# MLP up projection as seven half-size products a block, in blocks of 256 features, in a one-core trunk kernel

## What is computed

```python
z = rmsnorm(h, norm_mlp[l])                                     # 1024 x 1024
h = h + jnp.square(jax.nn.relu(z @ w_up[l])) @ w_down[l]        # w_up 1024 x 4096, w_down 4096 x 1024
...
return rmsnorm(h, norm_final)
```

## Time and profile before

| | |
|---|---|
| median of 3 runs | 1613.97 us |
| the profiled execution, its own time | 1612.35 us |
| its span in the profile | 1610.6 us |
| TensorE busy | 1550.3 us, 96% |
| VectorE, ScalarE, GpSimd busy | 756.5, 276.2, 408.2 us |
| the MLP's up and down matmuls | 3072, from about 896 to 1594 us |
| mean granted clock of TensorE | 0.989 of full speed |

### The profile page before, as it was taken

How to read it: one execution, slowest core, us unless ns; L and a number is a source line. 1 busy time by engine, 2 the same in 40 slices (tenths; PEclk the granted TensorE clock), 3 DMA queues, 4 the chain that set the end, 5 groups by cost and what they waited for, 6 DMA issues and landing times.

```text
span 1610.6 us, 20783 instructions
## 1 busy us (share of the span) xinstructions
PE 1550.3 (96%) x7608; PEld 1298.4 (81%) x7608; DVE 756.5 (47%) x1630; ACT 276.2 (17%) x575; POOL 408.2 (25%) x239
## 2 busy tenths in 40 slices
PE   5996999999999999999999999999999999999996
PEld 4785787878898988878888888888888888888884
DVE  6787665553564646476516622222232222222225
ACT  4120111220222222231102310101020101010013
POOL 1331132321010101104333306060513333240602
PEclk9997999999999999999999999999999999999998
DMA  5442344345211110103541103020211111020202
GB/s 167 117 120 72 93 117 119 105 158 164 72 41 39 34 44 26 53 27 125 170 170 53 53 1 105 0 92 13 65 39 52 52 47 58 26 78 0 91 0 104
DMA packets 93314, 119.16 MB, mean 74 GB/s; under 512 B 23504, under 2 KB 57424, under 8 KB 93264
## 3 DMA queue, kind: packets, MB, share of 16 engines
q1 hardware_dynamic: 62416, 78.49, 15.8%
q10 hardware_dynamic: 30848, 40.00, 7.8%
HBM read 96.57 MB, written 20.97 MB: 73 GB/s over the span
## 4 chain that ended last, share of the span: by engine, by line
PE 88%; DVE 7%; SPq 2%; issue 1%; ACT 1%; DMA 1%; ACTq 1%; POOL 0%; DVEq 0%
PE acc L497 27%; PE acc L499 27%; PE acc L498 27%; SPq L342 1%; PE aux L741 1%; DVE tb L1527 1%; PE aux L735 1%; PE aux L744 1%; DMA stage<-in_w_in 1%; PE aux L628 1%; ACTq L966 1%; PE aux L634 1%; DVE y_raw L1549 0%; SPq L339 0%; DVE tb L1574 0%
## 5 line engine op out<-in xcount | busy, mean ns | idle before, releaser
L421 POOL CAST w_hi<-stage 128x1024 fp32r<-128x1024 f32 x102 | 117.5, 1152 | 801.6 <-PE acc L499 674.3
L425 POOL TENSOR_TENSOR w_lo<-stage,w_hi 128x1024 fp32r<-128x1024 f32 x102 | 255.2, 2502 | 14.2 <-DVE x_in L1261 6.1
L497 PE MATMUL acc<-m_hi,w_hi 128*128 128x512 f32 x512 | 199.4, 390 | 0.0
L499 PE MATMUL acc<-m_hi,w_lo 128*128 128x512 f32 x512 | 199.2, 389 | 0.0
L498 PE MATMUL acc<-m_lo,w_hi 128*128 128x512 f32 x512 | 199.2, 389 | 0.0
L497 PE MATMUL acc<-w_hi,hid_hi 128*128 128x512 f32 x512 | 199.2, 389 | 0.0
L498 PE MATMUL acc<-w_lo,hid_hi 128*128 128x512 f32 x512 | 199.2, 389 | 0.0
L499 PE MATMUL acc<-w_hi,hid_lo 128*128 128x512 f32 x512 | 199.2, 389 | 0.0
L1797 DVE TENSOR_TENSOR h_res<-h_res,acc 128x512 f32<-128x512 f32 x128 | 87.9, 687 | 228.9 <-PE acc L499 228.9
L497 PE MATMUL acc<-w_hi,z_hi 128*128 128x256 f32 (+1 forms) x512 | 188.9, 369 | 0.0
L497 PE MATMUL acc<-z_hi,w_hi 128*128 128x512 f32 x448 | 179.8, 401 | 8.4 <-DVE z_lo L1221 5.0
(11 more groups left out here) (252 smaller groups left out, 2277.5 us busy)
## 6 DMA issues: line engine op xcount, KB each, us to landing
stage<-in_w_up SPq DMA_DIRECT2D x32, 512.0 KB, 3.7
stage<-in_w_down SPq DMA_DIRECT2D x32, 512.0 KB, 3.3
stage<-in_w_in SPq DMA_DIRECT2D x28, 512.0 KB, 3.8
gate_dram<-gate_t ACTq DMA_DIRECT2D x32, 256.0 KB, 2.0
x_in<-in_x SPq DMA_DIRECT2D x8, 512.0 KB, 8.1
stage<-in_w_in SPq DMA_DIRECT2D x32, 128.0 KB, 2.6
stage<-in_w_in SPq DMA_DIRECT2D x16, 256.0 KB, 3.1
gb_t<-gate_dram ACTq DMA_DIRECT2D x16, 256.0 KB, 3.1
```

The lines of the kernel that those rows point to most:

```text
L421: nc.gpsimd.tensor_copy(dst_hi, stage[:, s, :]).then_inc(hi_pool, 1)
L425: nc.gpsimd.tensor_tensor(dst_lo, stage[:, s, :], dst_hi.bitcast(F32), ALU.subtract)\
L497: nc.tensor.matmul(out, s_hi, m_hi_, start=first, stop=False)
L499: return nc.tensor.matmul(out, s_lo, m_hi_, start=False, stop=last)
```

## The change

Blocks are of 256 features, 16 in number. The first two are done in the plain way (4 up groups of 24 matmuls, 16 down groups of 6). The other 14 make the up projection by Strassen's seven products in Winograd's form: the z matrix is cut in four (feature half x position half), the weights of a block in four (feature half x 128 columns), and seven products of 512 x 128 x 512 (4 steps, 12 matmuls each) take the place of eight.

Sums of z quarters (S1 to S4) are made once: VectorE forms them during plain block 0 (`form_s1` to `form_s4`, each in two halves `u`), ScalarE casts and VectorE subtracts their parts during plain block 1. S1 takes the place of one quarter in `m_hi`, `m_lo`; the others lie where the weights of earlier stages were. Sums of weight quarters are made for each block by GpSimd, in `stage` and `t_sum`, and each of the seven weight operands (`piece`) is cast and subtracted into one of three slots of `t_hi`, `t_lo`. Product i goes to bank i % 4 of `aux`. ScalarE copies product 1 out; VectorE adds the others up in `tmp` and `c_tmp`, which gives four hidden quarters v, w, u, x in this order. The relu and the square become one VectorE operation. The down projection takes the positions' second half first (`DOWN_ORDER`).

The w_down part has buffers of its own (`dw_hi`, `dw_lo`); the same two slots of `stage` serve w_up and w_down. Waits: a piece waits for the product that used its slot; SyncE asks for w_down's halves after piece 4 and piece 7; the next block's w_up halves are asked for after w_down's halves are split.

The diff, cut to its core. The sizes and the order:

```diff
-FB = 512
+FB = 256
+N_PLAIN = 2
+DOWN_ORDER = (4, 5, 6, 7, 0, 1, 2, 3)
...
```

SyncE's loads of a seven-product block:

```diff
+            def load_block(g, first):
+                for i in range(2):
...
+                        sp.wait_ge(dn_ready, g * 2 + (i - 1))
+                    sp.dma_start(stage[:, i, :].rearrange("p (k c) -> p k c", k=KH),
+                                 w_up[:, KH * i:KH * i + KH, bass.ds(g * FB + N_PLAIN * FB, FB)]).then_inc(raw[i], 16)
+                for j in range(2):
+                    sp.wait_ge(t_ready, g * 7 + (4 if j == 0 else 7))
+                    sp.dma_start(stage[:, j, :].rearrange("p (k c) -> p k c", k=FT),
+                                 w_dn[:, bass.ds(g * FT + N_PLAIN * FT, FT), j * HALF:(j + 1) * HALF])\
+                      .then_inc(raw[j], 16)
...
```

GpSimd's part:

```diff
+                def piece(i, src):
+                    slot = i % 3
+                    pool.sem_inc(tick_pool, 1)
+                    pc.link(nc.gpsimd.tensor_copy(t_hi[:, slot, :, :], src))
+                    nc.gpsimd.tensor_tensor(t_lo[:, slot, :, :], src, t_hi[:, slot, :, :].bitcast(F32), ALU.subtract)\
+                      .then_inc(t_ready, 1)
+                pool.wait_ge(raw[0], g * 32 + 16 * (seen + 1))
+                pc.link(nc.gpsimd.tensor_tensor(b12, b12, b11, ALU.subtract))
...
+                piece(0, b11)
+                piece(1, t_sum[:])
...
+                piece(2, b11)
...
+                pool.wait_ge(prod, g * 7 + 1)
+                piece(3, b12)
+                pool.wait_ge(prod, g * 7 + 2)
+                piece(4, t_sum[:])
+                pool.wait_ge(prod, g * 7 + 3)
+                piece(5, b22)
+                pool.wait_ge(prod, g * 7 + 4)
+                piece(6, b21)
+                for j in range(2):
+                    pool.wait_ge(raw[j], g * 32 + 16 * (seen + 2))
...
+                    pc.link(nc.gpsimd.tensor_copy(hi, stage[:, j, :]))
+                    nc.gpsimd.tensor_tensor(lo, stage[:, j, :], hi.bitcast(F32), ALU.subtract).then_inc(dn_ready, 1)
...
```

TensorE's part:

```diff
+            def down(n0, h0, waits, order):
+                for j in range(2):
+                    for p, c in enumerate(order):
+                        n = n0 + 8 * j + p
+                        pe.wait_ge(out_free, n - 3)
+                        if j == 0 and p % 4 == 0:
+                            pe.wait_ge(lo_done, h0 + 2 + p // 2)
+                        if p == 0:
+                            pe.wait_ge(*waits[j])
...
+            def plain_block(f):
...
+                        if f == 0 and n in (OUT_MLP + 1, OUT_MLP + 2):
                             turn_z2(NCH - 3 + n - OUT_MLP)
-                        if half == 1 and q == 0:
+                        if f == 0 and half == 1 and q == 0:
                             pe.wait_ge(lo_done, SP_Z2 + 16)
...
+            def win_block(g, first):
...
+                for i, name in enumerate(("A11", "S2", "S3", "S1", "A22", "S4", "A12")):
+                    pe.wait_ge(t_ready, g * 7 + (i + 1))
+                    if i == 4:
+                        pe.wait_ge(p1_in, g + 1)
+                    if i > 4:
+                        pe.wait_ge(taken, g * 7 + (i - 4))
+                    for k in range(KH):
+                        mm = three(aux[:, i % 4, :], t_hi[:, i % 3, k, :], t_lo[:, i % 3, k, :],
+                                   a[name][0][:, k, :], a[name][1][:, k, :], k == 0, k == KH - 1)
+                    mm.then_inc(prod, 1)
...
```

VectorE's part (the sums of z, their place in plain block 0, and a block's adds, squares and low parts):

```diff
+            def form_s1(u):
+                link(V.tensor_tensor(raw_pair(s1_sum, u), z_pair(m_hi, 0, 1, u), z_pair(m_hi, 1, 1, u), ALU.add))
+                link(V.tensor_tensor(raw_pair(s_part, u), z_pair(m_lo, 0, 1, u), z_pair(m_lo, 1, 1, u), ALU.add))
+                V.tensor_tensor(raw_pair(s1_sum, u), raw_pair(s1_sum, u), raw_pair(s_part, u), ALU.add).then_inc(s_raw, 1)
...
+            def plain_block(f):
...
+                    if f == 0 and n < 2:
+                        form_s1(n)
+                    if f == 0 and n >= 2:
+                        form_s2(n - 2)
...
+                for j, p in down(n0 + 4, range(NCH)):
+                    if f == 0 and p % 4 == 3:
+                        (form_s3, form_s4)[j](p // 4)
...
+                add(u, x, 1)
...
+                add(w, u, 2)
...
+                add(v, w, 3)
+                add(u, u, 3)
+                square(v, 3)
+                dve.wait_ge(prod, n0 + 5)
+                add(w, w, 0)
+                square(w, 5)
+                lo(0, v, 1, 1)
+                dve.wait_ge(prod, n0 + 6)
+                add(u, u, 1)
+                square(u, 6)
+                lo(1, w, 0, 1)
+                dve.wait_ge(prod, n0 + 7)
+                add(x, x, 2)
+                square(x, 7)
+                lo(2, u, 1, 0)
+                lo(3, x, 0, 0)
```

More of the change, by code:

```diff
@@ L78 @@
 PER_HEAD = 10 * NCH
+PER_WIN = 13
 class Chain:
@@ L388, in _ @@
             w_dn = t["w_down"][0].rearrange("(k p) c -> p k c", p=P)
[L389 to L398, removed]
+            for f in range(N_PLAIN):
+                for i in range(2):
+                    load(LD_MLP + 4 * f + i, w_up[:, KH * i:KH * i + KH, f * FB:(f + 1) * FB], k=KH)
+                for j in range(2):
+                    load(LD_MLP + 4 * f + 2 + j, w_dn[:, FT * f:FT * f + FT, j * HALF:(j + 1) * HALF])
@@ L476, in _, with plain_split @@
                         regular(n, gr + j, i, g_slot + (n - LD_PB) // 2, OUT_PB + 8 * (gr + j - GR_PB) - 8)
[L477 to L483, removed]
-                              2 * i, f * 8 + (n + 1), freed=f * 24 + (OUT_MLP - 8 + 8 * b) if i == 0 else None)
+            def plain_split(n, dst_hi, dst_lo, done):
+                s = n % 2
+                pool.wait_ge(raw[s], 16 * (g_slot + (n - LD_PB) // 2 + 1))
+                nc.gpsimd.tensor_copy(dst_hi, stage[:, s, :]).then_inc(hi_pool, 1)
+                pool.wait_ge(hi_pool, done)
+                nc.gpsimd.tensor_tensor(dst_lo, stage[:, s, :], dst_hi.bitcast(F32), ALU.subtract)\
+                  .then_inc(w_ready, 1)
@@ L487, in _ @@
+            win_block(0, True)
+            with pool.Fori(1, N_WIN) as g:
+                pc.n = 0
+                pc.enter(g, PER_WIN)
+                win_block(g, False)
+                pc.leave(N_WIN - 1)
             pool.wait_ge(nf_in, 16)
-            for p, c in enumerate((1, 3, 5)):
+            for p, c in enumerate((DOWN_ORDER[1], DOWN_ORDER[3], DOWN_ORDER[5])):
                 pool.wait_ge(f_scaled, p + 1)
@@ L839, in mlp_block @@
+            def plain_block(f):
+                n0 = OUT_MLP + PLAIN_OUT * f
+                if f == 0:
+                    pe.wait_ge(lo_done, SP_Z2 + 8)
                 for half in range(2):
-                    for q in range(FB // P):
-                        n = OUT_MLP + 4 * half + q
-                        slot = GR_MLP % 2
-                        if first and n in (OUT_MLP + 1, OUT_MLP + 2):
+                    for q in range(FT):
+                        n = n0 + FT * half + q
+                        if f == 0 and n in (OUT_MLP + 1, OUT_MLP + 2):
@@ L875, in _ @@
+            for f in range(N_PLAIN):
+                plain_block(f)
+            win_block(0, True)
+            with pe.Fori(1, N_WIN) as g:
+                win_block(g, False)
         @block.scalar
```

334 lines of the change are left out of this document (252 added, 82 removed).

## The result

The changed kernel took 1660.34 us (median of 4 runs, 1657.32 to 1661.68) against 1613.63 of the kernel before (4 runs). The ratio is 1.0284, with a 95% interval of 1.0265 to 1.0303. The forecast was 1685 in a range of 1632 to 1713: sign, mechanism and range held, and the time came out 25 us lower, close to rival 1. The profiled execution took 1657.32 us (span 1655.5, before 1610.6).

What follows compares the result with a forecast made beforehand. TensorE was taken to bound the kernel. Matmuls -34.0, block waits +60, plain blocks +22, half clock +22 and +1 made +71 on 1612.35: 1683; the median, 1.6 higher, gave 1685 us, range 1632 to 1713.

Steps and rivals of the forecast that it cites:

- rival 1: Seven-product blocks: the waits come but the granted clock does not fall; 1662 us, chance 18%.
- Removed: MLP up projection: 168 matmuls go, 150 of them on the chain at 0.2266 us each; -34.0 us.
- Exclusion and turns: MLP: VectorE operations with two SBUF operands and GpSimd instructions exclude each other and alternate singly; it carried the 1685 us forecast.
- rival 2: Seven-product blocks: VectorE and GpSimd don't meet, down groups start at once, only block 0's 9 us stay; 1589 us, chance 8%.
- rival 3: VectorE's queued instruction overtakes a waiting GpSimd one; waits of 0.6 + 0.6 us a block; 1613 us, chance 8%.
- Rival 4: GpSimd becomes the bound if 512 columns cost as much as 1024: +12 us a block, above 1740 us, chance 6%.
- The wait in a block: Seven-product blocks: TensorE's first down group waits 4.3 us for VectorE's low part of w; x14 = +60 us.
- The clock: Behind each seven-product block's wait, some 3.4 us at half clock lose 1.6 us; 14 x 1.6 = +22 us.
- the sign that I had named: Seven-product blocks: granted clock below 1 in every block would show the forecast right; 1.6 us lost a block.
- The plain blocks: Two plain blocks: TensorE waits while VectorE forms the sums of z, +22 us, plus 1 for the clock.
- the z wait: Plain block 0, third up group: TensorE waits 2.1 us for the last transposed z.
- Hidden work: ScalarE's copies and the transfers stay hidden beside matmuls, ScalarE with more than 5 us of room; no time added.

Runs made afterwards that it cites:

- experiment 1: Changed kernel with GpSimd's split of w_down in the seven-product blocks cut to 8 of 1024 columns: 1599.39 us, ratio 0.9921 against the kernel before.
- experiment 7: Changed kernel with w's low part right behind v's on VectorE and GpSimd's second w_down half after all four low parts: 1601.37 us, ratio 0.9927.
- experiment 3: Changed kernel with VectorE making the low part of w right behind that of v, ahead of u's add and square: 1624.26 us, ratio 1.0071.
- experiment 5: Changed kernel with GpSimd's split of block 1's w_up cut to 8 of 1024 columns: 1654.01 us in one execution.
- experiment 6: Changed kernel with the sums of z formed later, S2 and S3 between block 0's down adds, S4 in block 1: 1664.77 us, ratio 1.0298.
- the best kernel: Changed kernel with w's low part early, GpSimd's second w_down half late, and the sums of z spread over both plain blocks: 1595.18 us, ratio 0.9883.
- experiment 4: Changed kernel with eight plain and eight seven-product blocks in place of 2 and 14, sums formed in the last two plain ones: 1656.59 us, ratio 1.0272.

## Why the prediction was right, step by step

**Removed, right.** Of 168 matmuls 150 were counted. The last fifth add of the second column half now stands at 1631.31, 24.2 us before the end of the span; before it was 1586.35, 24.25 before. The tail is the same, so the 18 matmuls behind that point saved nothing. Experiments 1 and 7 show the dense period of 40.80 that was computed.

**Exclusion and turns, right.** It carried the forecast, and experiments 1 and 3 show it: with GpSimd's four instructions small, all waits in the blocks go, and with all of them whole the place of one VectorE operation decides how long TensorE waits. Rivals 2 and 3 fall with it. In the block shown a VectorE operation runs at each change between GpSimd's four, and of those with two SBUF operands none overtakes a GpSimd instruction that waits, as in the earlier trace rows. The Trainium skill, "SBUF — State Buffer", section "SBUF: two separate sides", has the pair of ports locked for the whole instruction; that part the trace bears out (the low parts end 0.55 us behind GpSimd's). It gives the lock to whichever starts first, which leaves open who starts when both stand queued; here it was each in turn. Rival 4 falls by the rows: the 128x512 cast takes 0.61 us and the subtraction 1.29, against estimates of 0.60 and 1.27 for the step.

**The wait in a block, mis-sized: 3.15 us in place of 4.3.** The sequence of the prediction was met instruction by instruction. What was off is how long VectorE's operation holds GpSimd at each change of turns. I took 0.6 us a time, VectorE's step from start to start. The rows show GpSimd's casts at 1.50 over 1.04 and its subtractions at 2.75 and 2.66 over 2.40: 0.46 and 0.26 to 0.35. Over the four instructions that is 0.9 us: the low part of w ends at t = 11.33 and not 12.3. Counted in steps of 0.2266, as the forecast counted, product 7 ended at 8.16 as computed and the first down group started at 11.46: a wait of 3.30 in place of 4.3. The profile's 3.15 is the same wait, taken from the end of the last matmul's record, which lies 0.16 later; and the period loses 3.45, since the first matmul behind the wait takes a step of 0.33. With 3.45 lost per block and 2.2 in the first, the term is 47 and not 60.

**The clock, mis-sized: 7 us in place of 22.** The price of a dip was right (1.4 to 1.6 us for three, 2.7, the price I had given to a longer one, for the fourth). The count was not, and the sign that I had named, a granted clock below 1 in every block, did not come: at 4 of the 13 waits the clock fell to half, and not at the first block's 1.69. From the earlier trace rows I had waits of 2.59 and 3.43 with a dip and 2.33 without, and took every wait of 4.3 for one of the first kind. At 3.15 us that was true of 4 in 13; whether 4.3 us would lower it each time, no run shows. That the result lies near rival 1 is chance: its condition (no dip) is false, its 60 us of waits are 13 too many, and the dips and a late start make up for part of that. The forecast for the profiled execution was 1683, and it took 1657.3. Of the difference 13 us are the wait, 15 the clock and 2 the plain blocks; the 3.6 us by which the profiled run was late before block 0 count the other way.

**The plain blocks, right in sum.** +22 and +1 were forecast, +21.2 measured, with the fifth down group's 14.1 measured as 13.02, the z wait 1.57 for 2.1, the first down group 0.73 for 2.1, and 1.99 for the 2.2 between the adds. So the waits add up to 17.3 in place of some 22, and the sum fits because the clock took more than the 1 us counted: it was half to the end of the stretch shown, 949.65, and TensorE worked 4.7 us of that at half, which costs some 2.2 us. The rest is slower first steps behind the waits and what the list does not name. The turns, forecast at 11.6, were 5.8 and 3.9 by the reckoning of experiment 5.

**Hidden work, right.** No wait for GpSimd's pieces, for ScalarE or for a transfer appears in the blocks.

**What stays open.** Why a wait of 3.15 us lowers the clock after some blocks and not after others, though the work between is the same. In the profiles the dips come in groups of one to three, and the groups stand at different distances: 313 us here (1075 and 1388), 225 in experiment 5, 270 between the last two of experiment 6. No run here separates causes, and none was made in which only the clock could differ.

## What to carry to other kernels

When work moves to engines that have room in sum, place it in time before counting: list both engines' instructions from the event that releases them, let them alternate wherever VectorE reads two operands from SBUF (GpSimd's casts, which read one, take their turn too), and see when the one result that TensorE waits for comes out. Removing 150 matmuls was worth 34 us only once the second half of the neighbour's long instructions stood where VectorE had nothing but PSUM adds, and the critical low part stood ahead of the rest: two moved steps turned 1.028 into 0.993. Of the 34 us about 21 still went to the plain blocks, where the sums are formed, which is why the best kernel is only 1.2% faster than the one before. Behind a short repeated wait of a few microseconds count a clock loss as a range, not as a term, and prefer to remove the wait: the spread between runs goes with it.

## What the hardware showed beyond that

- A 128x512 GpSimd cast takes 0.61 us and a subtraction 1.29; at 1024 columns 1.04 and 2.40.
- The square in one operation that names its operand twice (L2075) is held by GpSimd like any with two SBUF operands: 1.46 and 0.81 in place of 0.69. The adds from PSUM (L2070) are not, in any block (98 of them, longest 0.69).
- In experiment 4 the 1.34 us waits of the plain blocks left the clock at 1.00 from 935 to 1200 us; at those of 3.15 us it fell sometimes; at that of 13 us in the changed kernel it was half from 936 to 949.65.
- The mean granted clock and the time of single executions go together: for the changed kernel 0.975, 0.974, 0.973, 0.972 with 1657.32, 1659.74, 1660.94, 1661.68.
